# Six weight tiles between the latent attention's heads multiplied as split operands instead of as full f32

## The chip, the cores and the metric

The kernel runs on one core of a Trainium2 chip. The metric is the device time of one execution in microseconds; lower is better.

## What is computed

Two transformer layers on 256 tokens of width 1024, batch 1, all in f32. The first layer is a four-branch mixer with a SwiGLU; the second is a mixer of a RWKV-7 time mix, a latent attention (MLA, 4 heads) and a gated delta net, with a squared-ReLU feed-forward. The change lies in the second layer, in the projection of its input:

```python
u = _rms(h, ln_mix_g[l])
p = u @ w_in[l]                      # 1024 -> P_IN, here "in2"
p_rwkv, p_mla, p_gdn = _split(p, (RWKV_IN, MLA_IN, GDN_IN))
y_rwkv = rwkv7_time_mix(p_rwkv, ...)
y_mla = mla_attention(p_mla, ...)    # 4 heads, softmax over 256 keys
y_gdn = gated_deltanet(p_gdn, ...)   # causal conv of 4 taps, silu, then the delta rule
```

## The kernel before, in words

Weights come in chunks of 16 KB a partition through a ring of three slots (`rings`). A product of a 128-column tile of weights with the 256 tokens runs over eight blocks of 128 input channels (`KD` = 8). There are two ways to do one:

- **full f32**: `product_f` (L619 to L626), eight matmuls of 256 columns straight from the ring slot and from `HT`, the normalised input. In the trace each shows as two records of L625.
- **split**: `product3` (L660 to L671). Weights and input are each kept as a rounded high part and a remainder (low part), both in the faster operand type fp32r, and each block takes three matmuls: high by high, high by low, low by high (L668). A split costs ScalarE one copy (the high part) and VectorE one subtraction (the low part) over all weights of the piece. `IN2_HIGH` and `IN2_LOW` hold the two parts of this layer's input.

The second layer's projection has seven chunks, `("in2", 0)` to `("in2", 6)`. Chunks 0, 1 and 2 are split in pieces of 2048 elements a partition. Chunks 3 to 6 are multiplied as full f32. Eight tiles, in chunks 4 and 5, belong to the delta net; a pair of tiles fills one PSUM bank and is one job. Six of them stand between the heads of the latent attention, as `filler(n)` with n from 0 to 5 (L1118 to L1125), so that TensorE has work while ScalarE and VectorE do a head's softmax. Chunk 5's last pair, `f_job("in2", 5, 1)`, follows the heads.

The order of work is written out by hand for each engine, and engines wait for one another on semaphores. What matters is this loop over `u` from `NU` to `NU + 4`; below, "turn 0" to "turn 4", with head 0 to 3.

- TensorE (L1130 to L1138): `filler(0)` ahead of the loop, then in each turn the scores of head u, the transposes of the probabilities of head u - 1 (L838), `filler(u + 1)`, and the values of head u - 1 (L844 to L846). After it come the spread rows (L1144), the last pair of tiles, and more.
- ScalarE (L1986 to L2007): in each turn the first tap of a convolution tile (L1664 stages a bank, L1693), the transposed probabilities of head u - 1 into SBUF (L1792), the exponentials of head u (L1782), the tanh of the convolution tile (L1701), and some small rows of the delta rule: Exp in turn 0, Ln in turn 1 (with a table load before it and one back to Exp behind), Exp in turn 2.
- VectorE (L2743 to L2754): in each turn the mask and row maximum of head u (`bias_scores`, L2370 and L2372), the other three taps of a convolution tile (L2252) and its product with the tanh (L2261), the division of head u - 1 (L2411, L2412), and rows of the delta rule (L2701 to L2725). Turn 0 has `key_factors` (L2731 to L2738) as well. After the loop the first instruction is L2757, which waits for the spread rows.

The later stretch that matters: TensorE builds the first matrices of the RWKV inverse (L1181 to L1209), VectorE masks them (L2966), and TensorE goes on (L1225, L1382).

Of the kernel before, what the change touches and what calls it, by code (L numbers as in the profile page):

```python
# [16 lines left out]
F32 = mybir.dt.float32  # L17
F32R = mybir.dt.float32r
I32 = mybir.dt.int32
ALU = mybir.AluOpType  # L20
# [193 lines left out]
def build(nc, x, weights, params, params2, consts, tables, rel_bias, norm_final, positions, table_dram, out):  # L214
    with ExitStack() as ctx:
# [5 lines left out]
        def sem(name):  # L221

            if name not in sems:
                sems[name] = ctx.enter_context(nc.semaphore(name))
            return sems[name]
# [9 lines left out]
        def over(name, place, at, shape):  # L235

            return nc.alloc_sbuf_tensor_at(name, [P] + shape, F32R, offset=places[place] + 4 * at)
# [20 lines left out]

        Y_RW_AT = (P2COL["uq"][0] + 7) // 8 * 8
        Y_RW_LOW, Y_MLA_LOW = over("Y_RW_LOW", "BIAS", Y_RW_AT, [3, S]), over("Y_MLA_LOW", "NF", 0, [2, S])  # L260
        OVER_HT, OVER_HN = over("OVER_HT", "HT", 0, [KD, S]), over("OVER_HN", "HN", 0, [KD, S])
        MIX_LOW = over("MIX_LOW", "ARENA", 17408, [KD, S])

# [162 lines left out]
        def wait_job_out(eng, job):  # L426

            j = JOB_AT[job]
            eng.wait_ge(sem(f"job_out{j % 4}"), j // 4 + 1)

        def piece_parts(k):

# [140 lines left out]
        def _(pe):  # L573
# [47 lines left out]
            def product_f(o, w, a, n=P, ks=range(KD)):  # L621

                for k in ks:
                    wait_operand(k)
                    ins = pe.matmul(o, w[:, k, a:a + n], HT[:, k, :], start=(k == 0), stop=(k == KD - 1))  # L625
                return ins  # L626
# [491 lines left out]
            def filler(n):  # L1118

                i, j, t = 4 + n // 4, n // 2 % 2, n % 2  # L1120
                w = chunk("in2", i, KD, 512)
                o = open_job(("in2", i, j)) if t == 0 else job_bank(("in2", i, j))
                ins = product_f(o[:, t * S:(t + 1) * S], w, (n % 4) * P)
                if t:
                    close_job(ins)  # L1125

# [440 lines left out]
        def _(act):  # L1567
# [362 lines left out]
            def shift_tiles(i, j, tiles):  # L1930

                shifts[0] += 1
                o = job_arrived(act, ("in2", i, j))
                k = len(stage_readers)
                act.wait_ge(sem(stage_readers[k - 2][0]), stage_readers[k - 2][1])
                stage_readers.append(("shift_by_dve", shifts[0]))
                n = len(tiles) * S
                act.activation(STG[:, k % 2, 0:n], o[:, 0:n], ACT.Copy)
                for n, rt in enumerate(tiles):
                    ins = act.activation(RZ[:, rt, :], o[:, n * S:(n + 1) * S], ACT.Copy, scale=one_minus_mu[:, rt:rt + 1])  # L1940
                job_out(ins, ("in2", i, j))
# [25 lines left out]
            def row_roots(name, rows, n, scale, eps):  # L1967

                o = fill_arrived(act, name)
                fill_out(act.activation(rows, o[0:HD, 0:n], ACT.Sqrt, bias=SMALL[eps][0:HD, :], scale=scale), name)  # L1970

            shift_tiles(3, 0, (8, 9))
            take_fill(("rw_g", 0), flat(GG[:, 0:2, :]), 512, 0.5)
            take_fill(("rw_g", 1), GG[:, 2, :], S, 0.5)
# [8 lines left out]
            for n, dst in enumerate((QTm, KTm)):  # L1983
                for b in range(2):
                    take_fill(("mla_T", 2 * n + b), flat(dst[0:QK, 2 * b:2 * b + 2, :]), 512, rows=QK)
            for u in range(NU, NU + MH + 1):  # L1986
                if NU < u < NU + MH:
                    conv_tap(u - NU + 7)
                if u > NU:
                    take_probs_T(u - 1)  # L1990
                if u < NU + MH:
                    exps(u)
                else:
                    conv_tap(11)
                if u > NU:
                    conv_tanh(u - NU + 7)
                if u == NU:
                    act.wait_ge(sem("sp_minus_abs"), 2)
                    act.activation(GSPT, GSPT, ACT.Exp).then_inc(sem("sp_exp"), 1)
                elif u == NU + 1:  # L2000
                    act.wait_ge(sem("sp_exp1"), 2)
                    act.activation(GSPT, GSPT, ACT.Ln).then_inc(sem("sp_ln"), 1)
                elif u == NU + 2:
                    act.wait_ge(sem("gdn_cumulated"), 1)
                    act.activation(EGCUM, GCUM, ACT.Exp)
                    act.activation(EKEND, GCUM[:, 0:P], ACT.Exp, bias=GCUM[:, P - 1:P], scale=-1.0)\
                        .then_inc(sem("gdn_rows"), 1)  # L2007
# [147 lines left out]
        def _(dve):  # L2155
# [201 lines left out]
            def bias_scores(u):  # L2357

                br, h = ALL_UNITS[u]
                dve.wait_ge(sem("scores_written"), u + 1)  # L2360
                if u >= 2:
                    dve.wait_ge(sem("probs_ready"), u - 1)
                o, s = BK[4 + u % 2], SB_[:, u % 2, :]
                if br == 0:
                    dve.tensor_tensor(s, o[:, 0:384], cst("ssd_mask"), ALU.add).then_inc(sem("scores_read"), 1)
                    return
                m = {1: HEAD_BIAS[:, h, :], 2: cst("causal"), 3: HEAD_BIAS[:, (0, 1, 4, 5, 2, 3, 6, 7).index(h), :],
                     4: cst("mla_mask")}[br]
                init = NSINK[:, h:h + 1] if br == 3 else 3e38
                dve.tensor_tensor_reduce(s[:, 0:P], o[:, 0:P], m[:, P:S], -1.0, init, ALU.add, ALU.min,  # L2370
                                         NEGM[:, u % 2, 0:1])
                dve.tensor_tensor_reduce(s[:, P:384], o[:, P:384], m, -1.0, init, ALU.add, ALU.min,  # L2372
                                         NEGM[:, u % 2, 1:2]).then_inc(sem("scores_read"), 1)
# [219 lines left out]
            def shift_tiles(i, j, tiles):  # L2593

                wait_job_out(dve, ("in2", i, j))
                o = STG[:, STAGED["in2", i, j] % 2, :]
                for n, rt in enumerate(tiles):
                    z = RZ[:, rt, 1:S]
                    ins = dve.scalar_tensor_tensor(out=z, in0=o[:, n * S:(n + 1) * S - 1], scalar=prm2("mu", rt), in1=z,
                                                   op0=ALU.mult, op1=ALU.add)  # L2600
                ins.then_inc(sem("shift_by_dve"), 1)
# [89 lines left out]
                                   bc(g4[:, :, HD - 1:HD], [P, 6, P]), ALU.subtract))  # L2691
            dve.tensor_tensor(E3[:, :, :], GM[:, :, :], LW[:, :, :], ALU.subtract).then_inc(sem("decay_sums"), 1)

            shift_tiles(3, 0, (8, 9))
            shift_tiles(3, 1, (10,))
            o = job_arrived(dve, ("in2", 3, 2))
            link(dve.tensor_copy(GAX, o[32:32 + RH, 0:S]))
# [45 lines left out]
            for u in range(NU, NU + MH + 1):  # L2743
                if u < NU + MH:
                    bias_scores(u)
                if u > NU:
                    conv_taps(u - NU + 7)
                    conv_out(u - NU + 7)
                if u > NU:
                    finish_head(u - 1)  # L2750
                delta_rule_rows(u)
                if u == NU:
                    key_factors()
# [515 lines left out]
```

## Time and profile before

| | before |
|---|---|
| median of 3 runs | 962.67 us (962.37 to 964.09) |
| the profiled execution | 964.36 us |
| its span in the trace | 962.6 us |
| TensorE matmul, busy | 940.6 us (98%) |
| VectorE, busy | 589.7 us (61%) |
| ScalarE, busy | 471.0 us (49%) |

The span runs from the first to the last instruction of the profiled execution; 1.76 us of its time lie around the span. Busy time of TensorE is a modelled figure: matmuls overlap, so the time between two starts says more than a duration.

### The profile page before, as it was taken

To read this page: it belongs to the slowest core of one execution; us is meant where nothing else is said; L and a number is where in the kernel's file an instruction comes from. 1 tells how busy PE (TensorE), PEld (TensorE's weight loads), DVE (VectorE), ACT (ScalarE), POOL (GpSimd) and SP (SyncE) were. 2 spreads that over 40 slices of the span, in tenths; PEclk is the share of its full clock that TensorE was granted. 3 is DMA by queue.
4 is the path that set the end of the run, shared out by engine and by line. 5 is a ranking of instruction groups with operands and counts; after the bars stand their busy time and mean duration, and the time that the engine had idled before them with its cause. 6 is when DMAs were issued, how large, how long until landed. Compare 5 with 4: busy or idle time off the path is not lost.

```text
span 962.6 us, 16894 instructions
## 1 busy us (share of the span) xinstructions
PE 940.6 (98%) x7147; PEld 832.6 (86%) x7147; DVE 589.7 (61%) x931; ACT 471.0 (49%) x706; POOL 62.9 (7%) x76
## 2 busy tenths in 40 slices
PE   6999999999999999999999999999999999999998
PEld 5999987787778789999988899788988789998886
DVE  4775445557678755555553749578777466665434
ACT  5644335546773454444443665456335455545331
POOL 1000000021003300000000010002260000000000
PEclk9999999999999999999999989999999999999999
DMA  9985552243446534455553442222000444455521
GB/s 354 203 319 196 193 198 101 91 142 143 159 176 253 195 113 175 176 186 191 197 208 123 176 154 89 89 88 88 4 2 3 175 176 175 176 184 190 217 109 44
DMA packets 14778, 149.86 MB, mean 156 GB/s; under 512 B 1696, under 2 KB 3872, under 8 KB 6128
## 3 DMA queue, kind: packets, MB, share of 16 engines
q1 hardware_dynamic: 12448, 139.65, 39.0%
q0 software_dynamic: 1296, 5.24, 2.9%
q10 hardware_dynamic: 960, 3.90, 1.0%
q8 instruction: 57, 0.93, 0.4%
q14 instruction: 17, 0.14, 0.0%
HBM read 144.59 MB, written 4.19 MB: 155 GB/s over the span
## 4 chain that ended last, share of the span: by engine, by line
PE 85%; DVE 6%; ACT 4%; issue 2%; POOL 1%; ACTq 0%; DVEq 0%; POOLq 0%
PE bank L668 64%; PE bank L625 5%; PE bank L1382 3%; DVE W_LOW L2208 2%; ACT W_HIGH L1643 2%; PE bank L797 1%; POOL HN L3087 1%; PE bank L838 1%; PE bank L875 1%; PE bank L1144 1%; DVE ARENA L2252 1%; DVE X L2514 1%; PE bank L1249 1%; DVE OUT_LOW L2208 0%; PE bank L634 0%
## 5 line engine op out<-in xcount | busy, mean ns | idle before, releaser
L2208 DVE TENSOR_TENSOR W_LOW<-weights,W_HIGH 128x2048 fp32r<-128x2048 f32 (+1 forms) x98 | 224.4, 2292 | 214.0 <-ACT W_HIGH L1643 214.0
L1643 ACT ACTIVATE W_HIGH<-weights 128x2048 fp32r<-128x2048 f32 (+1 forms) x98 | 186.7, 1907 | 264.7 <-PE bank L668 264.7
L668 PE MATMUL bank<-OVER_HT,W_HIGH 128*128 128x256 f32 x608 | 171.0, 281 | 0.3 <-DVE OVER_HN L2220 0.3
L668 PE MATMUL bank<-OVER_HT,W_LOW 128*128 128x256 f32 x608 | 170.5, 280 | 0.0
L668 PE MATMUL bank<-OVER_HN,W_HIGH 128*128 128x256 f32 x608 | 170.5, 280 | 0.0
L668 PEld LDWEIGHTS bank<-OVER_HT,W_HIGH 128*128 128x128 f32 x608 | 114.5, 188 | 1.0 <-issue 0.8
L668 PEld LDWEIGHTS bank<-OVER_HN,W_HIGH 128*128 128x128 f32 x608 | 114.5, 188 | 0.0
L668 PEld LDWEIGHTS bank<-OVER_HT,W_LOW 128*128 128x128 f32 x608 | 114.5, 188 | 0.0
L668 PE MATMUL bank<-W_LOW,HID_HIGH 128*128 128x512 f32 x200 | 77.9, 389 | 0.0
L668 PE MATMUL bank<-W_HIGH,HID_LOW 128*128 128x512 f32 x200 | 77.9, 389 | 0.0
L668 PE MATMUL bank<-W_HIGH,HID_HIGH 128*128 128x512 f32 x200 | 77.8, 389 | 0.0
L668 PE MATMUL bank<-FIRST_HIGH,W_HIGH 128*128 128x256 f32 x224 | 63.6, 284 | 1.9 <-DVE W_LOW L2208 1.4
L668 PE MATMUL bank<-FIRST_HIGH,W_LOW 128*128 128x256 f32 x224 | 63.4, 283 | 0.0
L668 PE MATMUL bank<-FIRST_LOW,W_HIGH 128*128 128x256 f32 x224 | 63.3, 282 | 0.0
L625 PE MATMUL bank<-HT,weights 128*128 128x256 f32 x240 | 55.4, 383 | 0.0
L668 PE MATMUL bank<-GATE_HIGH,FIRST_HIGH 128*128 128x512 f32 x128 | 52.5, 410 | 0.5 <-DVE RING_LOW L2348 0.5
L668 PE MATMUL bank<-RING_LOW,FIRST_HIGH 128*128 128x512 f32 x128 | 50.3, 393 | 0.0
L668 PE MATMUL bank<-GATE_HIGH,FIRST_LOW 128*128 128x512 f32 x128 | 50.2, 392 | 0.0
L625 PEld LDWEIGHTS bank<-HT,weights 128*128 128x128 f32 x240 | 44.5, 190 | 6.7 <-issue 0.7
L2348 DVE TENSOR_TENSOR RING_LOW<-weights,GATE_HIGH 128x1024 fp32r<-128x1024 f32 x32 | 40.7, 1272 | 11.9 <-ACT GATE_HIGH L1678 11.9
L668 PEld LDWEIGHTS bank<-FIRST_HIGH,W_HIGH 128*128 128x128 f32 x224 | 42.3, 189 | 3.3 <-DVE W_LOW L2208 1.8
L668 PEld LDWEIGHTS bank<-W_HIGH,HID_HIGH 128*128 128x128 f32 x200 | 37.5, 188 | 7.8
(509 smaller groups left out, 1887.4 us busy)
## 6 DMA issues: line engine op xcount, KB each, us to landing
weights<-weights_dram SPq DMA_DIRECT2D x63, 2048.0 KB, 7.9
bias_rows_dram<-ARENA POOLq DMA_DIRECT2D x1, 3072.0 KB, 40.9
weights<-weights_dram SPq DMA_DIRECT2D x2, 1024.0 KB, 5.9
BIAS<-params_dram ACTq DMA_DIRECT2D x1, 1997.0 KB, 14.5
weights<-weights_dram SPq DMA_DIRECT2D x1, 1664.0 KB, 6.8
weights<-weights_dram SPq DMA_DIRECT2D x1, 1584.0 KB, 6.9
X<-x_dram ACTq DMA_DIRECT2D x2, 512.0 KB, 4.3
HT<-bias_rows_dram POOLq DMA_DIRECT2D x1, 1024.0 KB, 10.9
```

The lines of the kernel that those rows point to most:

```text
L625: ins = pe.matmul(o, w[:, k, a:a + n], HT[:, k, :], start=(k == 0), stop=(k == KD - 1))
L668: ins = pe.matmul(o, left[a][k], right[b][k], start=(first and k == 0 and a + b == 0), stop=(last and k == n - 1 and a == 1))
L797: ins = pe.matmul(BK[4 + u % 2][:, c0:c1], q[:, q0:q0 + P], k[:, 0:n], start=True, stop=(br != 2))
L838: ins = pe.transpose(probsT_bank(u)[:, j * P:(j + 1) * P], PB_[:, u % 2, j * P:(j + 1) * P], ident)
L875: ins = pe.matmul(o[pb:pb + HD, c0:S], V[:, n, a:a + HD], PT_[:, u % 2, k0:k1], start=(n == 0), stop=(n == 1))
L1144: ins = pe.matmul(o[:, c * P:(c + 1) * P], at[0:HD, :], rows, start=True, stop=True)
L1249: ins = pe.matmul(o[pb:pb + HD, c * P:(c + 1) * P], a[:, c, h * HD:(h + 1) * HD], b[:, matrix(c, h), :], start=(n == 0), stop=(c == 0 and ...
L1382: ins = pe.matmul(o[b:b + HD, n * HD:(n + 1) * HD], left[b:b + HD, 4 * g + n, :], right[b:b + HD, 4 * g + n, :], start=True, stop=True)
L1643: act.activation(like_source(piece_parts(k)[0], k), piece_source(k), ACT.Copy).then_inc(sem("pieces_high"), 1)
L2208: dve.tensor_tensor(low, piece_source(k), high.bitcast(F32), ALU.subtract)\
L2252: ins = dve.scalar_tensor_tensor(out=a, in0=o[:, 0:S - d], scalar=w[tap], in1=a, op0=ALU.mult, op1=ALU.add)
L2348: dve.tensor_tensor(low, src, high.bitcast(F32), ALU.subtract).then_inc(sem("gate_split"), 1)
```

## The change

For tiles n = 0 to 5 (`IN_TILES` = 6) `filler(n)` uses `product3` instead of `product_f`. A tile's high part is copied by ScalarE into one of two buffers (`TILE_HIGH`, 1024 elements a partition each), its low part is written by VectorE over the tile's own weights in the ring slot.

```diff
+        IN_TILES = 6
+        TILE_HIGH = [over("TILE_HIGH0", "HN", 0, [KD, P]), over("TILE_HIGH1", "BIAS", Y_RW_AT, [KD, P])]
...
+        def in_tile(n):
+            slot = weight_slots("in2", 4 + n // 4)[0]
+            cols = slice(n % 4 * P, (n % 4 + 1) * P)
+            src, low = [t[:, :].rearrange("p (k n) -> p k n", k=KD)[:, :, cols] for t in (rings[slot], RING_LOW[slot])]
+            return TILE_HIGH[n % 2], low, src
+
+        def wait_tile_read(eng, n):
+            if n % 2:
+                eng.wait_ge(sem("jobs_written"), JOB_AT["in2", 4 + n // 4, n // 2 % 2] + 1)
+            else:
+                eng.wait_ge(sem("tiles_read"), n // 2 + 1)
...
@@ TensorE, filler(n)
-                ins = product_f(o[:, t * S:(t + 1) * S], w, (n % 4) * P)
+                if n < IN_TILES:
+                    pe.wait_ge(sem("tiles_split"), n + 1)
+                    ins = product3(o[:, t * S:(t + 1) * S], [[part[:, k, :] for k in range(KD)] for part in in_tile(n)[0:2]],
+                                   [[part[:, k, :] for k in range(KD)] for part in stream2])
+                    if t == 0:
+                        ins.then_inc(sem("tiles_read"), 1)
+                else:
+                    ins = product_f(o[:, t * S:(t + 1) * S], w, (n % 4) * P)
@@ ScalarE
+            def tile_high(n):
+                slot, turn = weight_slots("in2", 4 + n // 4)
+                act.wait_ge(sem(f"weights_in{slot}"), 16 * turn)
+                if n >= 2:
+                    wait_tile_read(act, n - 2)
+                high, _, src = in_tile(n)
+                act.activation(high[:, :, :], src, ACT.Copy).then_inc(sem("tiles_high"), 1)
+
+            for n in range(2):
+                tile_high(n)
             shift_tiles(3, 0, (8, 9))
...
             for u in range(NU, NU + MH + 1):
+                if u < NU + IN_TILES - 2:
+                    tile_high(u - NU + 2)
                 if NU < u < NU + MH:
                     conv_tap(u - NU + 7)
@@ VectorE
+            def tile_low(n):
+                dve.wait_ge(sem("tiles_high"), n + 1)
+                high, low, src = in_tile(n)
+                dve.tensor_tensor(low, src, high[:, :, :].bitcast(F32), ALU.subtract).then_inc(sem("tiles_split"), 1)
+
             shift_tiles(3, 0, (8, 9))
+            for n in range(2):
+                tile_low(n)
             shift_tiles(3, 1, (10,))
...
                 if u < NU + MH:
                     bias_scores(u)
+                if u < NU + IN_TILES - 2:
+                    tile_low(u - NU + 2)
                 if u > NU:
                     conv_taps(u - NU + 7)
```

Where this moves instructions shows at three places. In the changed kernel the lines are some tens higher (L1643 to L2007 become L1666 to L2043, L2252 becomes L2288, L2370 becomes L2406); `TILE_HIGH_57` and `_58` are the two buffers, `RING_LOW_50` and `_51` the ring slots of chunks 4 and 5.

TensorE, `filler(0)` and what follows it, before:

```order
L625 MATMUL bank<-HT,weights 128x256 [waits job_out1,weights_in1]
L625 MATMUL bank<-HT,weights 128x256 x7
L797 MATMUL bank<-ARENA 128x128 [waits fill_out7,fill_out6,scores_read,fill_out5,fill_out4]
L797 MATMUL bank<-ARENA 128x256
L625 MATMUL bank<-HT,weights 128x256 [waits weights_in1]
```

and in the changed kernel, the first of eight blocks and the next tile's start:

```order
L684 MATMUL bank<-IN_HIGH,TILE_HIGH_57 128x256 [waits tiles_split,job_out1,weights_in1]
L684 MATMUL bank<-IN_LOW,TILE_HIGH_57 128x256
L684 MATMUL bank<-IN_HIGH,RING_LOW_50 128x256
...
L813 MATMUL bank<-ARENA 128x128 [waits fill_out7,fill_out6,scores_read,fill_out5,fill_out4]
L813 MATMUL bank<-ARENA 128x256
L684 MATMUL bank<-IN_HIGH,TILE_HIGH_58 128x256 [waits tiles_split,weights_in1]
```

Eight matmuls of a tile become 24, and each tile's first one waits for VectorE's subtraction. The scores keep their place.

ScalarE, from the Ln of turn 1 to the first convolution tap of turn 3, before (the last row is in turn 3):

```order
L2002 ACT_TABLE_LOAD
L2002 ACTIVATE SM<-SM 6x256
L1693 ACTIVATE ARENA<-bank,BIAS 128x256
L1792 ACTIVATE ARENA<-bank 128x384
L1782 ACT_TABLE_LOAD
L1782 ACTIVATE ARENA,STAT<-ARENA,STAT 128x128
L1782 ACTIVATE ARENA,STAT<-ARENA,STAT 128x256
L1701 ACTIVATE ARENA<-ARENA 128x256
L2005 ACTIVATE SM<-SM 6x256
L2006 ACTIVATE SM<-SM 6x128
L1664 ACTIVATE ARENA<-bank 128x512
```

and in the changed kernel:

```order
L2038 ACT_TABLE_LOAD
L2038 ACTIVATE SM<-SM 6x256
L2002 ACTIVATE TILE_HIGH_57<-weights 128x1024
L1716 ACTIVATE ARENA<-bank,BIAS 128x256
L1815 ACTIVATE ARENA<-bank 128x384
L1805 ACT_TABLE_LOAD
L1805 ACTIVATE ARENA,STAT<-ARENA,STAT 128x128
L1805 ACTIVATE ARENA,STAT<-ARENA,STAT 128x256
L1724 ACTIVATE ARENA<-ARENA 128x256
L2041 ACTIVATE SM<-SM 6x256
L2042 ACTIVATE SM<-SM 6x128
L2002 ACTIVATE TILE_HIGH_58<-weights 128x1024
```

The copy of the next tile but one comes first in each turn, ahead of the tap, of the transposed probabilities and of the exponentials; the copies of tiles 0 and 1 stand ahead of the loop.

VectorE, turn 1, before:

```order
L2370 ISA ARENA,STAT<-bank,CST 128x128
L2370 ISA STAT 128x1
L2372 ISA ARENA,STAT<-bank,CST 128x256
L2372 ISA STAT 128x1
L2252 SCALAR_TENSOR_TENSOR ARENA<-ARENA,BIAS 128x255
```

and in the changed kernel:

```order
L2406 ISA ARENA,STAT<-bank,CST 128x128
L2406 ISA STAT 128x1
L2408 ISA ARENA,STAT<-bank,CST 128x256
L2408 ISA STAT 128x1
L2734 TENSOR_TENSOR RING_LOW_50<-weights,TILE_HIGH_58 128x8x128
L2288 SCALAR_TENSOR_TENSOR ARENA<-ARENA,BIAS 128x255
```

The subtraction stands behind the row maxima and ahead of the taps, in each of turns 0 to 3. POOL's and SP's instructions do not move.

## Rows read from the trace of the kernel before

**Rows 1.** The page: busy us of each engine, its share of the span, its instructions

```profile
PE 940.6 (98%) x7147; PEld 832.6 (86%) x7147; DVE 589.7 (61%) x931; ACT 471.0 (49%) x706; POOL 62.9 (7%) x76
```

**Rows 2.** Windows around the loop: window, then busy us of PE, PEld, DVE, ACT, POOL, granted clock

```profile
609.00:621.10 12.10, 12.10 (x82) 8.90 (x81) 1.65 (x4) 5.68 (x12) 0.00 (x0) 1.00 0.42 154
621.10:645.20 24.10, 24.10 (x138) 21.69 (x137) 17.93 (x57) 14.86 (x39) 0.00 (x0) 1.00 0.26 98
645.20:674.80 29.60, 27.70 (x260) 23.35 (x259) 26.58 (x56) 17.27 (x39) 6.25 (x9) 1.00 0.19 73
```

**Rows 3.** Timeline of TensorE: start, us, instruction; a split product's 24, then fillers 0 and 1

```profile
570.91 0.28 PE L668 MATMUL bank<-IN_HIGH,W_HIGH 128*128 128x256 f32 x1
...
573.67 0.28 PE L668 MATMUL bank<-IN_HIGH,W_LOW 128*128 128x256 f32 x1
...
616.70 3.62 PE L625 MATMUL bank<-HT,weights 128*128 128x256 f32 x16
...
620.81 3.62 PE L625 MATMUL bank<-HT,weights 128*128 128x256 f32 x16
```

**Rows 4.** Lines L1678 and L2348: copy and subtraction of 1024 elements, ns min/median/max

```profile
L1678 ACT ACTIVATE GATE_HIGH<-weights x32: 1040/1057/1062, 136.2 to 270.6; 128x1024 fp32r<-128x1024 f32 x32
L2348 DVE TENSOR_TENSOR RING_LOW<-weights,GATE_HIGH x32: 1214/1224/1777, 139.2 to 274.4; 128x1024 fp32r<-128x1024 f32 x32
```

**Rows 5.** Timeline of VectorE: its rows behind a wait [idle before <-releaser], and one more

```profile
612.43 0.48 DVE L2599 SCALAR_TENSOR_TENSOR ARENA<-ARENA,BIAS 128x255 f32<-128x255 f32 x1 [3.43 <-ACT ARENA L1940]
...
621.11 0.29 DVE L2370 CUSTOM_DVE_ANT_0 ARENA<-bank,CST 128x128 f32<-128x128 f32 x1 [4.86 <-PE bank L797]
...
626.06 0.28 DVE L2370 CUSTOM_DVE_ANT_0 ARENA<-bank,CST 128x128 f32<-128x128 f32 x1
...
628.61 0.42 DVE L2261 SCALAR_TENSOR_TENSOR ARENA<-ARENA 128x256 f32<-128x256 f32 x1 [0.48 <-ACT ARENA L1701]
...
629.52 0.17 DVE L2411 RECIPROCAL STAT<-STAT 128x2 f32<-128x2 f32 x1 [0.49 <-PE bank L846]
...
631.04 1.52 DVE L2252 SCALAR_TENSOR_TENSOR ARENA<-ARENA,BIAS 128x255 f32<-128x255 f32 x3 [0.16 <-ACT ARENA L1693]
...
634.30 0.42 DVE L2261 SCALAR_TENSOR_TENSOR ARENA<-ARENA 128x256 f32<-128x256 f32 x1 [1.75 <-ACT ARENA L1701]
...
638.19 1.52 DVE L2252 SCALAR_TENSOR_TENSOR ARENA<-ARENA,BIAS 128x255 f32<-128x255 f32 x3 [1.07 <-ACT ARENA L1693]
...
640.20 0.42 DVE L2261 SCALAR_TENSOR_TENSOR ARENA<-ARENA 128x256 f32<-128x256 f32 x1 [0.48 <-ACT ARENA L1701]
...
643.69 0.43 DVE L2261 SCALAR_TENSOR_TENSOR ARENA<-ARENA 128x256 f32<-128x256 f32 x1 [0.48 <-ACT ARENA L1701]
...
645.23 1.14 DVE L2757 TENSOR_TENSOR ARENA<-ARENA,bank 128x512 f32<-128x512 f32 x2 [0.59 <-PE bank L1144]
```

**Rows 6.** Timeline of ScalarE: the gap ahead of the loop, then turns 1 and 2

```profile
605.49 0.60 ACT L1938 ACTIVATE ARENA<-bank 128x512 f32<-128x512 f32 x1 [5.09 <-PE bank L625]
...
628.59 1.28 ACT L2002 ACT_TABLE_LOAD   x1
630.23 0.42 ACT L2002 ACTIVATE SM<-SM 6x256 f32<-6x256 f32 x1 [0.36 <-DVE SM L2711]
...
631.18 0.49 ACT L1792 ACTIVATE ARENA<-bank 128x384 f32<-128x384 f32 x1 [0.17 <-ACT ARENA L1693]
631.68 1.28 ACT L1782 ACT_TABLE_LOAD   x1
...
636.62 0.42 ACT L2005 ACTIVATE SM<-SM 6x256 f32<-6x256 f32 x1 [2.35 <-DVE SM L2718]
```

**Rows 7.** Who TensorE waited for from 597 to 675 us, longest: us, times, longest us

```profile
PE bank L1225 <- DVE ARENA L2966: 1.3, 1, 1.3
```

**Rows 8.** Windows where TensorE's work was thin, columns as in rows 2

```profile
564.00:568.00 4.00, 4.00 (x20) 4.00 (x21) 0.00 (x0) 2.23 (x3) 0.00 (x0) 0.50 0.01 4
708.00:712.00 4.00, 2.51 (x68) 2.17 (x64) 2.61 (x6) 1.42 (x4) 2.25 (x4) 1.00 0.00 0
```

## The prediction

> **What bounds the kernel now.** I read the page first: TensorE is busy for 98% of the span, VectorE for 61% and ScalarE for 49% [rows 1]. That makes the change look like a plain gain, less TensorE time for work on engines with room. But these are shares of the whole span. So I read the windows around the attention loop next [rows 2]. From 621.1 to 645.2 us VectorE is busy 17.93 of 24.10 us and ScalarE 14.86. From 645.2 to 674.8 VectorE is busy 26.58 of 29.60 us, and TensorE then waits 1.3 us for VectorE at L1225 [rows 7], its longest wait from 597 us on. So in this part TensorE is only just the bound: VectorE's list is nearly as long. The third view, VectorE's timeline [rows 5], shows how near. At the loop's end VectorE waited only 0.59 us for TensorE (L2757, at 645.23). What it idled inside the loop it mostly idled for ScalarE.
>
> **What TensorE gains.** A full-f32 tile takes 3.46 us: 3.62 us of rows, less 0.16 of overlap, since the 16 records from 616.70 are followed at 620.15 by the next work, and the next such group starts at 620.81 [rows 3]. A split tile takes 24 matmuls. The first and the last of the 24 of a split product start at 570.91 and 573.67: they stand (573.67 - 570.91) / 23 = 0.120 us apart [rows 3], so a tile takes 24 x 0.120 = 2.88 us. The gain is 0.58 us a tile, 3.5 us for six. The Trainium skill ("TensorE: Matmul & The Clock Gate", Back-to-back issue gap) gives an isolated matmul at full clock N / 2.4 + 2.5 ns, 109 ns at 256 columns. By it, as an estimate, a tile would take 2.6 us. The rows at full clock show 120 ns, so the trace does not agree, and the sum takes the row; by the page's figure it would come out 0.3 us lower, as an estimate.
>
> **What ScalarE and VectorE pay.** Six copies and six subtractions of 1024 elements a partition. The nearest rows are the same two operations on the first layer's gate pieces: 1.06 us and 1.22 us, median of 32 each [rows 4]. Sources there are two runs of 512 elements; here they are eight runs of 128, 2 KB apart, which no row shows. From below, the same price; from above, the slowest of the 32 subtractions, 1.78 us. I take 1.0 us for a copy (its start-to-start share) and 1.25 for a subtraction, near the median, since nothing in the rows makes the stride dear. A hand-over between engines I take as 0.04 us.
>
> **Tiles 0 and 1: free.** ScalarE sits idle for 5.09 us before 605.49 [rows 6] and both copies fit there; chunk 4's weights have landed long before. VectorE sits idle for 3.43 us before 612.43 [rows 5] and two subtractions, 2.5 us, fit there. TensorE needs tile 0 at 616.70. If that cover were gone, `filler(0)` would be late by what sticks out.
>
> **Tiles 2 to 5: not free.** These four lie in turns 0 to 3. VectorE does 4 x 1.25 = 5.0 us more between 621.11 and 645.23. It starts 0.58 us earlier, since the scores of head 0 come after a shorter `filler(0)`. What can pay for the rest are the waits it has there [rows 5]: 0.48 + 0.49 + 0.16 + 1.75 + 1.07 + 0.48 + 0.48 + 0.59 = 5.5 us. The question is which of them last. Three (0.48 each) are the tanh of a convolution tile, which starts only when VectorE's taps end: these stay whatever happens. The 0.49 and the 0.59 are for TensorE, and go. The others hang on ScalarE's order, so I walked through the two lists with the durations above and those of the timelines, every instruction starting when its engine is free and its releaser done:
>
> - Turn 0. Row maxima at 620.5, tile 2's low part to 622.4, then `key_factors`; the next row maxima come at 626.8 where they came at 626.06 [rows 5].
> - Turn 1, and ScalarE's start of turn 2. Row maxima to 627.4, tile 3 to 628.7, taps to 630.2, tanh on ScalarE to 630.6. Only then does ScalarE load the Ln table (1.28 us [rows 6]), do the Ln (632.3), and copy tile 4 (633.3). Behind that copy stand the tap, the probabilities of head 1 into SBUF (done at 633.9, before at 631.67 [rows 6]), the second table load, and the exponentials of head 2.
> - Turn 2. VectorE waits 0.8 us for tile 4's copy, and 0.7 us for the tanh where it was 1.75. TensorE, ready for the values of head 1 at 631.5, gets them at 633.9: a stall of 2.4 us, and 0.9 us more for the next probabilities.
> - Turn 3. ScalarE does its two Exp rows when VectorE's scan is done, at about 639 (before 636.62 [rows 6]), then tile 5's copy to 640.6. VectorE waits 1.1 us for it; TensorE's values of head 2 stall 2.6 us, since their probabilities come behind that copy, and the next probabilities 0.3 us.
>
> VectorE's waits come to about 0.5 + 0.8 + 0.7 + 1.1 + 0.5 + 0.5 = 4.1 us in place of 5.5. So L2757 starts later by 5.0 - 0.58 - 1.4 = 3.0 us. TensorE's side gives the same from its own numbers: new stalls 2.4 + 0.9 + 2.6 + 0.3 = 6.2 us, less 3.5 us of shorter products: 2.7 us late at the spread rows. The two differ since VectorE need not wait 0.6 us at L2757 any more, and by roundings.
>
> **Behind the loop** nothing gives it back. TensorE's and VectorE's lists are both late by about the same, VectorE is 90% busy up to 674.8 [rows 2], and TensorE's 1.3 us wait at L1225 [rows 7] lasts. After that the chain is TensorE's again and slides whole. DMAs have cover: slots are freed a few us later, and the next chunks in them belong to the layer's output projection, well behind the delta net.
>
> **Sum:** +2.7 us on the profiled execution's 964.36 us (span 962.6, 1.8 us around it) gives 967.1. That execution lies 1.7 us above the median of the runs shown, 962.67, so against the median: **965.4 us**. About 0.2%, 1.9 us, is what a measurement of this kernel can tell from no change. Bounds of the unknown: with 1.78 us a subtraction the same walk gives +4.7; with 1.22 and 1.0, +2.6.
>
> **Rivals.**
>
> 1. *The splits are covered* (faster). VectorE's idle 5.5 us does hold 5.0 us of work, and by the page both helpers are far from full [rows 1]. If ScalarE's copies came into gaps (it idles 9 us in the loop [rows 2]) and no one waited for them, only TensorE's gain would count: -3.5 us, 959.2. Against: the copies stand at each turn's head, ahead of what TensorE waits for, and VectorE's end had 0.59 us to spare. It decides if the four subtractions delay L2757 by less than that. Chance 0.11.
> 2. *A draw*: the waits for ScalarE close up more than in my walk, leaving only the tanh waits, 4 x 0.48. VectorE's end then is late by 5.0 - 0.6 - 3.6 = +0.8 us, so 963.5, within 0.2%. For it: my walk carries some 30 hand-overs, each uncertain by 0.05. Chance 0.26.
> 3. *The clock falls.* At 564 to 568 us the granted clock was 0.50, 1.2 of 2.4 GHz, after TensorE had done 32-column products; from 708 to 712, with 2.51 us busy of 4 and waits between, it stayed at 1.00 [rows 8]. New stalls of 2.5 us are of the second kind. If the clock fell for some 7 us as it did there, about two tiles would double, +4 us on top: 969.4. The Trainium skill ("TensorE: Matmul & The Clock Gate", What's actually happening) says that the array is throttled by default and that activity releases it, which would let a stalled loop fall back; rows 8 show both outcomes. Chance 0.05.
>
> Slower as walked: 0.58.
>
> **How the numbers follow.** Faster by over 0.2%: rival 1, with 0.11. Within 0.2%: rival 2, with 0.26. Slower: 0.58 + 0.05 = 0.63. The range runs from 961.5 (a little of rival 1, which alone reaches 959.2) to 967.8 (most of the dear subtraction); outside are most of rival 1, the clock, and the tail of the price, together 2 in 10.
>
> **What the profile after would show.** Right: split tiles of 2.9 us on TensorE; copies near 1.0 and subtractions near 1.25 us; TensorE waiting for ScalarE's L1792 and L1782 (by their new numbers) some 6 us in all in the loop, where it waited for nothing; L2757 some 3 us later. Wrong if those waits are missing, or if VectorE still waits for TensorE at L2757; then rival 1 holds. A granted clock below 1 between 630 and 650 us would be rival 3. If the loop ends 3 us late and the span does not, something behind it had slack that I did not see.

## The result, and the profile after

| | before | after |
|---|---|---|
| first measurement, median (runs) | 962.67 us (7) | 967.09 us (7) |
| ratio after to before, 95% interval | | 1.0038 (1.0022 to 1.0053) |
| the same two kernels measured again (`c1`) | 965.04 us (22) | 967.74 us (12) |
| ratio, 95% interval | | 1.0025 (1.0013 to 1.0036) |
| the profiled execution, and its span | 964.36, 962.6 us | 966.05, 964.2 us |

The change makes the kernel slower, by 4.4 us between the medians of the first measurement (3.7 by the ratio, 2.1 to 5.1 by its interval) and by 2.7 us in the second, with its narrower interval of 1.3 to 3.5. The forecast was 965.4 us, within 961.5 to 967.8; the first measurement has 967.09.

The page after, the counterpart of [rows 1]:

```profile
PE 939.7 (97%) x7195; PEld 833.6 (86%) x7195; DVE 595.7 (62%) x937; ACT 477.5 (50%) x712; POOL 63.1 (7%) x76
```

VectorE has six instructions and 6.0 us more, ScalarE six and 6.5. TensorE has 48 records more (six tiles of 24 where there were 16) and 0.9 us less, although the new tiles save more than that. Where the rest went shows in the windows around the loop, columns as in [rows 2] (the last one is 3.2 us longer):

```profile
609.00:621.10 12.10, 12.10 (x102) 9.52 (x101) 4.48 (x12) 6.22 (x15) 0.00 (x0) 1.00 0.48 174
621.10:645.20 24.10, 21.08 (x149) 20.01 (x148) 19.27 (x52) 15.08 (x34) 0.00 (x0) 0.86 0.24 89
645.20:678.00 32.80, 30.87 (x330) 26.45 (x331) 29.29 (x64) 19.78 (x45) 6.25 (x9) 1.00 0.18 65
```

From 621.1 to 645.2 us TensorE was busy all 24.10 us before; now it is idle for 3.0 of them, and the granted clock, 1.00 before, is 0.86. Both points were in the prediction, the first as the forecast, the second as rival 3.

Whom TensorE waited for from 590 to 690 us (us in all, times, longest), to be held against [rows 7]:

```profile
PE bank L860 <- ACT ARENA L1815: 2.3, 1, 2.3
PE bank L1248 <- DVE ARENA L3012: 1.3, 1, 1.3
PE bank L854 <- ACT ARENA L1805: 0.7, 1, 0.7
```

L860 is the values of a head, L1815 its transposed probabilities on ScalarE; L854 and L1805 are the transposes and the exponentials. L1248 is L1225 before, with its 1.3 us unchanged. The waits of the loop are the two forecast for head 1 (2.4 and 0.9 us); those forecast for head 2 (2.6 and 0.3) are missing.

The two helpers' new instructions, ns min/median/max and span of the six:

```profile
L2002 ACT ACTIVATE TILE_HIGH<-weights x6: 1038/1062/1119, 598.7 to 638.0; 128x1024 fp32r<-128x1024 f32 x6
L2734 DVE TENSOR_TENSOR RING_LOW<-weights,TILE_HIGH x6: 1217/1222/1226, 607.4 to 639.1; 128x1024 fp32r<-128x1024 f32 x6
```

They cost what the contiguous ones in [rows 4] cost: eight runs of 128 elements, 2 KB apart, are not dear. VectorE's timeline (start, us, instruction, idle before it and its releaser), against [rows 5]:

```profile
607.36 2.35 DVE L2734 TENSOR_TENSOR RING_LOW<-weights,TILE_HIGH 128x1024 fp32r<-128x1024 f32 x2
610.88 0.48 DVE L2635 SCALAR_TENSOR_TENSOR ARENA<-ARENA,BIAS 128x255 f32<-128x255 f32 x1 [1.17 <-ACT ARENA L1963]
...
618.98 0.29 DVE L2406 CUSTOM_DVE_ANT_0 ARENA<-bank,CST 128x128 f32<-128x128 f32 x1 [4.29 <-PE bank L813]
...
628.76 0.42 DVE L2297 SCALAR_TENSOR_TENSOR ARENA<-ARENA 128x256 f32<-128x256 f32 x1 [0.48 <-ACT ARENA L1724]
...
631.43 1.23 DVE L2734 TENSOR_TENSOR RING_LOW<-weights,TILE_HIGH 128x1024 fp32r<-128x1024 f32 x1 [1.11 <-ACT TILE_HIGH L2002]
...
635.06 0.42 DVE L2297 SCALAR_TENSOR_TENSOR ARENA<-ARENA 128x256 f32<-128x256 f32 x1 [0.97 <-ACT ARENA L1724]
...
639.06 1.23 DVE L2734 TENSOR_TENSOR RING_LOW<-weights,TILE_HIGH 128x1024 fp32r<-128x1024 f32 x1 [1.19 <-ACT TILE_HIGH L2002]
...
646.45 1.13 DVE L2803 TENSOR_TENSOR ARENA<-ARENA,bank 128x512 f32<-128x512 f32 x2
```

The subtractions of tiles 0 and 1 (the first row) took up idle time: 3.43 us of it before the next tap have become 1.17. The last row is the old L2757 (645.23): it no longer waits for TensorE. The waits between the row maxima of head 0 and that row are 0.48, 1.11, 0.97, 1.19 and twice 0.48 us, 4.7 in all, where 4.1 were forecast and 5.5 stood before.

ScalarE's timeline in the same columns, from the Ln of turn 1 to the copy of turn 3, against [rows 6]:

```profile
628.75 1.28 ACT L2038 ACT_TABLE_LOAD   x1
630.04 0.41 ACT L2038 ACTIVATE SM<-SM 6x256 f32<-6x256 f32 x1
630.36 1.04 ACT L2002 ACTIVATE TILE_HIGH<-weights 128x1024 fp32r<-128x1024 f32 x1
...
631.93 0.49 ACT L1815 ACTIVATE ARENA<-bank 128x384 f32<-128x384 f32 x1 [0.17 <-ACT ARENA L1716]
632.44 1.28 ACT L1805 ACT_TABLE_LOAD   x1
...
637.37 0.41 ACT L2041 ACTIVATE SM<-SM 6x256 f32<-6x256 f32 x1 [2.35 <-DVE SM L2762]
...
637.99 1.04 ACT L2002 ACTIVATE TILE_HIGH<-weights 128x1024 fp32r<-128x1024 f32 x1
```

Tile 4's copy stands between the Ln and the probabilities of head 1, which TensorE's 2.3 us wait is for; they are 0.75 us later than in [rows 6], though the whole stretch started 1.55 us earlier.

**One measure for all traces.** Executions differ before the loop: the transposes ahead of it (L1115; `filler(0)` comes behind them) start at 614.91 us in the trace before, at 613.36 in the one after, and at 611.84 in a second trace of the changed kernel. So each trace is measured from there to the counterpart of L2757 ("loop") and to TensorE's start behind the wait at the counterpart of L1225 ("to L1225"), both in us; "walk" is what a walk through ScalarE's and VectorE's lists gave for the loop against before, in the prediction (by VectorE's list 3.0, by TensorE's 2.7) and in the expectations. The walks of the experiments were written down before each ran, but with the trace of the changed kernel already at hand.

| trace | loop | against before | walk | to L1225 | rest of the span |
|---|---|---|---|---|---|
| before | 30.32 | | | 59.88 | 287.8 |
| after | 33.09 | +2.77 | +2.7 to +3.0 | 62.63 | 288.2 |
| e1, two tiles | 29.38 | -0.94 | -1.2 | 59.09 | 288.2 |
| e2, splits without their use | 34.11 | +3.79 | +3.9 | 63.70 | 288.7 |
| e3, products alone | 28.76 | -1.56 | -1.8 | 58.31 | 288.8 |
| e4, four tiles | 32.29 | +1.97 | +1.3 | 61.85 | 288.8 |
| e5, kept running | 33.09 | +2.77 | | 62.65 | 288.8 |
| e6, subtractions on GpSimd | 37.23 | +6.91 | +0.4 | 66.80 | 289.2 |
| e7, four copies later | 35.83 | +5.51 | +5.3 | 65.39 | 289.1 |
| c1, the change again | 33.09 | +2.77 | | 62.65 | 289.2 |
| e8, kept running twice | 33.09 | +2.77 | | 62.65 | 289.2 |

By this table the two profiled spans differ by -1.55 (start) + 2.75 (to L1225) + 0.40 (rest) = 1.6 us. The middle term is the change's. As for the last one, the rest of the span is 0.4 to 1.4 us longer than before in every other trace, with longer and shorter loops alike; why is not shown.

### The profile page after: what moved, and what is told of

Same layout as the page of the kernel before. It is cut to its first block, busy times and chain, and to the rows that moved or that the text cites. A ratio compares the mean times of both kernels' runs of the same rounds, so it can differ in the third digit from the quotient of the medians.

```text
span 964.2 us, 17009 instructions
## 1 busy us (share of the span) xinstructions
PE 939.7 (97%) x7195; PEld 833.6 (86%) x7195; DVE 595.7 (62%) x937; ACT 477.5 (50%) x712; POOL 63.1 (7%) x76
## 4 chain that ended last, share of the span: by engine, by line
PE 83%; DVE 7%; ACT 5%; issue 2%; POOL 1%; ACTq 0%; DVEq 0%; POOLq 0%
PE bank L684 65%; PE bank L641 3%; PE bank L1405 3%; DVE W_LOW L2244 2%; ACT W_HIGH L1666 2%; POOL HN L3133 1%; PE bank L813 1%; PE bank L854 1%; DVE ARENA L2288 1%; PE bank L891 1%; PE bank L1167 1%; DVE X L2550 1%; PE bank L1272 1%; DVE OUT_LOW L2244 0%; PE bank L650 0%
## 5 line engine op out<-in xcount | busy, mean ns | idle before, releaser
L1666 ACT ACTIVATE W_HIGH<-weights 128x2048 fp32r<-128x2048 f32 (+1 forms) x98 | 186.7, 1907 | 262.6 <-PE bank L684 262.6
L684 PEld LDWEIGHTS bank<-W_HIGH,HID_LOW 128*128 128x128 f32 x200 | 37.5, 188 | 7.9
L684 PEld LDWEIGHTS bank<-W_LOW,HID_HIGH 128*128 128x128 f32 x200 | 37.5, 188 | 7.8
```

The costliest lines, as they stand in the source:

```text
L684: ins = pe.matmul(o, left[a][k], right[b][k], start=(first and k == 0 and a + b == 0), stop=(last and k == n - 1 and a == 1))
L1666: act.activation(like_source(piece_parts(k)[0], k), piece_source(k), ACT.Copy).then_inc(sem("pieces_high"), 1)
```

## The experiments

**One: two tiles only.** The free splits without the others.

```diff
-        IN_TILES = 6
+        IN_TILES = 2
```

> Only tiles 0 and 1 are split (IN_TILES = 2), whose copies and subtractions lie in gaps ahead of the loop. Theory 1 (the lists of VectorE and ScalarE inside the loop set its length): TensorE is 1.15 us shorter, nothing is added inside the loop, L2757's counterpart comes 1.2 us earlier after the first filler's start than in the kernel before, and the time is 1.2 us below the kernel before. Theory 2 (the clock's fall after the new stalls is the main price): no new stall, so no fall, the same 1.2 us gain. Theory 3 (the split product itself is slow in this place: operands out of the ring in 128-column pieces, or a switch between operand types): +0.3 to +1 us, two tiles at over 3.5 us each.

Measured: 964.39 us against 964.25, ratio 1.0005 (0.9993 to 1.0018). In the trace the loop is 0.94 us shorter and TensorE has no new wait. The splits of tiles 0 and 1 are free, and their gain shows in the trace of the loop. It does not show in the time: the interval, -0.7 to +1.7 us, leaves the 0.94 us just out. The mean granted clock of these runs was a little lower (0.995 in the median, 0.996 for the kernel before), which may hide it; whether the gain arrives at the end is open.

**Two: all splits, their result not used.** The products stay full f32; the copies and subtractions of the change are all made, each subtraction written over its own copy, and ScalarE waits for it before the buffer's next copy.

```diff
-                    ins = product3(o[:, t * S:(t + 1) * S], [[part[:, k, :] for k in range(KD)] for part in in_tile(n)[0:2]],
-                                   [[part[:, k, :] for k in range(KD)] for part in stream2])
+                    ins = product_f(o[:, t * S:(t + 1) * S], w, (n % 4) * P)
...
+                    act.wait_ge(sem("tiles_split"), n - 1)
...
-                dve.tensor_tensor(low, src, high[:, :, :].bitcast(F32), ALU.subtract).then_inc(sem("tiles_split"), 1)
+                dve.tensor_tensor(high[:, :, :], src, high[:, :, :].bitcast(F32), ALU.subtract).then_inc(sem("tiles_split"), 1)
```

> All six tiles are copied and subtracted as in the change, and TensorE waits for each, but multiplies them as full f32 out of the ring; the subtraction's result goes over the copy and is not used. Theory 1: the whole price without the gain, by the walk through the lists +3.9 us against the kernel before (1.2 us worse than the walk gave for the change, since head 0's scores come 0.6 us later and so on). Theory 2: TensorE is busier, its stalls are shorter (2.4 us less 0.6 or so each), and if the clock does not fall the time is below that of the change, near +2. Theory 3: the price is in the product, so +0.5 at most.

Measured: 968.05 us, ratio 1.0042 (1.0026 to 1.0059). TensorE's waits in its trace, as above:

```profile
PE bank L860 <- ACT ARENA L1814: 2.1, 2, 1.5
PE bank L854 <- ACT ARENA L1804: 0.7, 1, 0.7
```

The loop is 3.79 us longer: the price of the splits alone. With the shorter products it is 2.77. So six tiles that are each 0.58 us shorter bring 1.0 us of their 3.5.

**Three: the shorter products, without the splits of tiles 2 to 5.** Those four multiply what stands in the buffers of tiles 0 and 1, so the results are not the layer's; only the time is of use.

```diff
-                    pe.wait_ge(sem("tiles_split"), n + 1)
-                    ins = product3(o[:, t * S:(t + 1) * S], [[part[:, k, :] for k in range(KD)] for part in in_tile(n)[0:2]],
+                    pe.wait_ge(sem("tiles_split"), min(n + 1, 2))
+                    parts = in_tile(n)[0:2] if n < 2 else (TILE_HIGH[n % 2], TILE_HIGH[1 - n % 2])
+                    ins = product3(o[:, t * S:(t + 1) * S], [[part[:, k, :] for k in range(KD)] for part in parts],
...
-                if u < NU + IN_TILES - 2:
-                    tile_high(u - NU + 2)
...
-                if u < NU + IN_TILES - 2:
-                    tile_low(u - NU + 2)
```

> Tiles 2 to 5 are multiplied as three products of what is left in the two buffers of tiles 0 and 1; their own copies and subtractions are left out. Theory 1: all of the shorter products, nothing added in the loop: TensorE is 3.5 us shorter, but VectorE's and ScalarE's lists in the loop then set its end, so only 1.8 us are gained, not 3.5; TensorE shows some 1.7 us of new waits. Rival to it (TensorE alone bounds the loop): -3.5 us. Theory 3: no gain or a loss.

Measured: 962.18 us against 964.25, ratio 0.998 (0.997 to 0.999), 2.1 us between the medians and 1.56 us in the loop. TensorE's waits:

```profile
PE bank L860 <- ACT ARENA L1816: 1.2, 1, 1.2
PE bank L854 <- ACT ARENA L1806: 0.2, 1, 0.2
```

Even with four splits left out, the 3.5 us are not to be had: TensorE now outruns ScalarE, and the loop's end goes by the helpers' lists (VectorE no longer waits for TensorE there). Rival 1's 959.2 us was out of reach whatever the splits cost.

**Four: four tiles.**

```diff
-        IN_TILES = 6
+        IN_TILES = 4
```

> Four tiles are split (IN_TILES = 4): two inside the loop instead of four. Theory 1: +1.3 us against the kernel before, half of the way between two tiles (-1.2) and six (+2.7) or a bit over. Theory 2: the stall of turn 2 (tile 4's copy ahead of the probabilities) is gone or short, so the clock stays at 1.00 and the time is at most +0.5.

Measured: 965.69 us, ratio 1.0016 (1.0003 to 1.0029), loop +1.97 where the walk had +1.3. Tiles 4 and 5 are full f32 again, and at the loop's end VectorE waits for TensorE, 0.63 us in the row here and 0.59 us more at the old L2757:

```profile
644.57 0.17 DVE L2447 RECIPROCAL STAT<-STAT 128x2 f32<-128x2 f32 x1 [0.63 <-PE bank L862]
```

The granted clock has a part in this. The windows from 630 to 640 us:

```profile
630.00:635.00 5.00, 2.92 (x17) 2.22 (x16) 2.63 (x9) 3.87 (x10) 0.00 (x0) 0.92 0.77 265
635.00:640.00 5.00, 5.00 (x22) 4.19 (x21) 3.31 (x11) 3.20 (x10) 0.00 (x0) 0.73 0.37 156
```

Filler 4, full f32 here, starts at 634.21 us and took 5.30 us, where such a tile takes 3.62 with the clock up. Behind it TensorE has no wait up to the instruction that VectorE waits for (L862, at 644.15 us). It used the probabilities of head 2 at 639.35 us; ScalarE had them ready at 638.34. So with the clock up TensorE would have been some 1 us earlier from there on. That is an estimate from these rows, and more than the 0.7 us that the walk lacks; no execution of this kernel without the fall was traced.

**Five: is it the clock?** Ten idle products keep TensorE busy where it waits for the probabilities of head 1.

```diff
+                if u == NU + 2:
+                    keep_running(10)
```

> The change with 10 dummy 128-column f32 matmuls behind filler 3 (turn 2), where TensorE stalled 2.3 us for the probabilities of head 1: they last about 2.2 us, inside the stall. Theory 1: the loop's length does not hang on TensorE there, so the end of the loop is where it is in the change, or earlier by what the slow tile cost, 0 to 0.5 us. Theory 2 (clock): the granted clock stays at 1.00 from 634 to 641 us, filler 4 takes 2.9 us and not 5.1, and over the runs the time is 1 to 2 us below the change's, +2.7 against the kernel before.

Measured: 967.89 us against 963.62, ratio 1.0043 (1.0027 to 1.006); the gain of 1 to 2 us on the change that the clock theory asked for did not come. The windows from 634 to 641 us after the change, and here:

```profile
634.00:641.00 7.00, 6.29 (x31) 6.23 (x31) 4.71 (x15) 4.65 (x15) 0.00 (x0) 0.51 0.42 177
```

```profile
634.00:641.00 7.00, 4.33 (x34) 4.00 (x34) 4.81 (x14) 4.57 (x14) 0.00 (x0) 1.00 0.40 167
```

The clock stays up in this execution, and the loop takes the same 33.09 us. What changed is how TensorE spends that time. In the chain of waits after the change (start, us, engine, output, line), filler 4 takes 5.12 us, the next one 2.83:

```profile
635.67 5.12 PE bank L684 x24
...
641.85 2.83 PE bank L684 x24
```

With the clock up, in experiment five, it takes about 2.9, and the values behind it wait 2.1 us for their probabilities:

```profile
PE bank L860 <- ACT ARENA L1817: 2.1, 1, 2.1
PE bank L854 <- ACT ARENA L1807: 0.7, 1, 0.7
```

That is the wait of head 2 that the prediction had and the trace after lacks: TensorE at half clock filled it: its values of head 2 start at 640.59 us, 0.35 us behind the end of the copy of their probabilities.

**Six: the subtractions of tiles 2 to 5 on GpSimd,** which is idle in the loop.

```diff
-                if u < NU + IN_TILES - 2:
-                    tile_low(u - NU + 2)
...
+            for n in range(2, IN_TILES):
+                pool.wait_ge(sem("tiles_high"), n + 1)
+                high, low, tile = in_tile(n)
+                pool.tensor_tensor(low, tile, high[:, :, :].bitcast(F32), ALU.subtract).then_inc(sem("tiles_split"), 1)
```

> The change with the subtractions of tiles 2 to 5 on GpSimd (2.67 us each by its one row of this size in the trace before) instead of VectorE; ScalarE's copies stay. Theory 1: 5 us leave VectorE's list, the copies stay in ScalarE's: by the walk +0.4 us against the kernel before. If VectorE's part of the price is nothing and the copies' order is all, it stays at +2.7. If GpSimd and VectorE disturb one another, VectorE's instructions grow longer beside the GpSimd ones and the time lies above +1.

Measured: 972.47 us (6 runs), ratio 1.0082 (1.0059 to 1.0105): far dearer than the change, and the walk, +0.35 for +6.91, refuted. The timeline of GpSimd and VectorE shows most of it:

```profile
621.24 2.39 POOL L3157 TENSOR_TENSOR RING_LOW<-weights,TILE_HIGH 128x1024 fp32r<-128x1024 f32 x1 [49.62 <-ACT TILE_HIGH L2002]
...
621.29 2.49 DVE L2750 TENSOR_SCALAR SM<-SM 6x256 f32<-6x256 f32 x1
...
625.59 2.38 POOL L3157 TENSOR_TENSOR RING_LOW<-weights,TILE_HIGH 128x1024 fp32r<-128x1024 f32 x1 [1.96 <-ACT TILE_HIGH L2002]
625.70 3.08 DVE L2779 SCALAR_TENSOR_TENSOR ARENA<-ARENA 128x768 f32<-128x768 f32 x1
```

For comparison, the same two VectorE instructions after the change:

```profile
620.68 0.27 DVE L2750 TENSOR_SCALAR SM<-SM 6x256 f32<-6x256 f32 x1
...
622.88 0.96 DVE L2779 SCALAR_TENSOR_TENSOR ARENA<-ARENA 128x768 f32<-128x768 f32 x1
```

An instruction of VectorE that starts behind GpSimd's ends only after it: 0.27 us becomes 2.49, 0.96 becomes 3.08. It is the same in turns 2 and 3, where three taps take 3.37 and 2.87 us for 1.52. So VectorE is relieved of 1.2 us a tile and charged between 1.35 (2.87 - 1.52) and 2.2 us (2.49 - 0.27): 7.5 us in all for 4.9. That is 2.6 of the 4.1 us by which this loop is longer than the changed kernel's. VectorE's waits grew by 1.1 us as well, most of it for the first taps on ScalarE (1.47 and 2.02 us), and for 0.37 us it waited for TensorE at the end, where the clock was 0.66 from 645 to 650 us.

**Seven: ScalarE's order.** Four tiles, with the copy behind the exponentials in place of ahead of the tap.

```diff
-        IN_TILES = 6
+        IN_TILES = 4
...
             for u in range(NU, NU + MH + 1):
-                if u < NU + IN_TILES - 2:
-                    tile_high(u - NU + 2)
...
+                if u < NU + IN_TILES - 2:
+                    tile_high(u - NU + 2)
```

> Four tiles as in e4_four_tiles, the same work on each engine, but in each turn ScalarE's copy stands behind the exponentials instead of ahead of the tap. Theory 1 (order, not amount): VectorE's subtraction, and all behind it in its list, waits for the exponentials, so by the walk +5.3 us against the kernel before, 4 us worse than four tiles with the copy first. A theory of amounts alone (busy time added to busy engines) gives the same time as e4_four_tiles.

Measured: 969.47 us (6 runs), ratio 1.0056 (1.0034 to 1.0077), loop +5.51 where the walk had +5.27. It is the work of experiment four in another order, 3.5 us dearer in the loop. VectorE's two subtractions show where:

```profile
623.32 1.23 DVE L2734 TENSOR_TENSOR RING_LOW<-weights,TILE_HIGH 128x1024 fp32r<-128x1024 f32 x1 [2.00 <-ACT TILE_HIGH L2002]
...
631.49 1.23 DVE L2734 TENSOR_TENSOR RING_LOW<-weights,TILE_HIGH 128x1024 fp32r<-128x1024 f32 x1 [2.00 <-ACT TILE_HIGH L2002]
```

The exponentials depend on VectorE's row maxima, so a copy behind them comes a whole exchange later, and VectorE stands in front of its subtraction for 2.00 us. In four the copy was done before VectorE came to it.

**Eight: the change again, and with the clock held up in both gaps.** The second kernel has experiment five's line and ten idle products behind filler 4 as well:

```diff
+                if u == NU + 3:
+                    for _ in range(10):
+                        pe.matmul(job_bank(("in2", 5, 0))[:, S:S + P], ident, ident, start=True, stop=True)
```

> The changed kernel, once more, beside the next one on the same chip. The stretch from the first transposes to L2757 in its trace is 33.1 us as before (30.3 in the kernel before), +2.8. If falls of the clock outside this stretch make up the rest of the measured +3.7 to +4.4 us, the trace or the mean granted clocks of the runs (0.991 in the median, 0.996 in the kernel before) show more time at half clock than the loop's 7 us; if the clock has no part in it, the ratio falls to that of +2.8 us, 1.003.

> As e5_kept_running, and 10 dummy matmuls behind filler 4 as well, where the next stall (2.1 us, for the probabilities of head 2) came in that run's trace. If the rest of the loss over the lists' +2.8 us is the clock's fall after that second stall, the runs' median granted clock goes up to 0.996, and the time is +2.8 to +3.2 us against the kernel before. If it stays at +4.2, the rest is not the clock of this loop.

Measured side by side: the change 967.74 us, ratio 1.0025 (1.0013 to 1.0036); kept running twice 967.71 us, ratio 1.0026 (1.0015 to 1.0037). The windows of the change's second trace, then of the other kernel's:

```profile
629.00:634.00 5.00, 2.67 (x14) 1.96 (x15) 3.05 (x6) 4.30 (x9) 0.00 (x0) 0.81 0.87 308
634.00:641.00 7.00, 5.91 (x43) 5.57 (x43) 5.15 (x15) 4.50 (x13) 0.00 (x0) 0.89 0.19 81
```

```profile
629.00:634.00 5.00, 4.21 (x34) 3.62 (x33) 2.98 (x6) 4.37 (x10) 0.00 (x0) 1.00 0.90 301
634.00:641.00 7.00, 7.00 (x60) 6.82 (x60) 5.15 (x16) 4.44 (x13) 0.00 (x0) 1.00 0.21 88
```

Once the clock falls in the loop and once it does not; the loop is 33.09 us both times. Over the twelve runs of each, the mean granted clock rose from 0.9935 to 0.995 in the median, and the times are equal. With six tiles, the clock in the loop has no part in the price.

## Why the prediction was right, and where it was not

**TensorE's gain: right in size, in part out of reach.** Filler 0 of the changed kernel runs from 615.07 to 618.03 us in its trace, hand-over and all, and 24 products stand 0.120 us apart, so 2.88 us a tile. Of the 3.5 us for six, experiment three shows 1.6 in the loop as the most that it passes on. The prediction's remark that tiles of 2.6 us would lower the sum by 0.3 us counts one tile; on TensorE's side of the sum six make 1.6 (6 x 0.26), of which the first tile's share alone starts VectorE's list earlier.

**Copies and subtractions: right.** 1.06 and 1.22 us, for 1.0 and 1.25. The dear end, 1.78 us, did not occur.

**Tiles 0 and 1 free: right.** VectorE's idle time shrank from 3.43 to 1.17 us there, and ScalarE's 5.09 us gap to 3.19; experiment one has no price at all in the loop.

**Tiles 2 to 5 not free: right, by the mechanism named.** VectorE starts the loop's work early by the forecast 0.58 us: its first row maxima come 6.20 us behind the transposes before (621.11 - 614.91) and 5.62 after (618.98 - 613.36). Its waits go from 5.5 to 4.7 us (forecast 4.1), and the old L2757 comes 2.8 us later (forecast 3.0 by VectorE, 2.7 by TensorE). TensorE's stalls for head 1 are 2.3 and 0.7 us for 2.4 and 0.9. Experiment two isolates the price of the splits, 3.79 us for the walk's 3.9, and experiment seven moves one instruction a turn and gets 5.51 for 5.3.

**The stalls of head 2: not in the trace after, for a reason that the prediction had put elsewhere.** They were forecast at 2.6 and 0.3 us; the trace has none. The granted clock fell to 0.51 instead, filler 4 took 5.12 us in place of 2.9, and ended about when the probabilities came. With the clock up (experiment five) the wait is there, 2.1 us. Rival 3 is thus half right: the clock fell in both traces of the changed kernel, so a chance of 0.05 for the fall was far too low, but its step "+4 us on top" is wrong. It added the slow tiles to stalls that the slow tiles replace. Here 2 us of slowness fell on an engine that would have waited 2.1 us, and were free. In experiment four, where the slow tile was a full-f32 one and the wait behind it would have been shorter, part of it most likely was not.

**Behind the loop nothing gives it back: right.** The 2.77 us are 2.75 at the counterpart of L1225, and its own wait is 1.3 us as before.

**The sum.** Against the median it was +2.7 us. The second measurement has 2.7, the traces' loops 2.8, the first measurement 4.4, 1.7 above the forecast. No term of the walk is behind that 1.7: kernels with the same 33.09 us loop came out at 967.09 to 967.89 us, and the kernel before at medians of 962.67 (also over seven runs), 964.25, 963.62 and 965.04. So 967.09 lies 1.7 us above the 965.4 by the low level of the kernel before in that measurement, and the range held it by 0.7 us; with the level of the second measurement the same +2.7 gives 967.7, which is what was measured there. The kernel before's single executions in these measurements reach from 960.8 to 968.4 us. They go with the granted clock: over its 73 runs beside the experiments, each held against the mean of its own measurement, an execution is 0.8 us longer for each 0.001 that its mean granted clock is lower (correlation -0.81). Whether that carries the 1.7 us is not shown.

**Rivals 1 and 2.** Rival 1's condition, subtractions that delay L2757 by less than 0.59 us, failed by the 2.8. Rival 2, the draw, needed the waits for ScalarE to close up to the tanh waits alone; two waits for copies (1.11 and 1.19 us) and 0.5 us of a tanh that came late behind one stayed. What none of the rivals had is a subtraction put where it is not in VectorE's way; experiment six tried that and fell to another resource.

**A better version** was not found. Two tiles are 0.9 us shorter in the loop and equal in time (1.0005). Not tried: a third buffer for high parts, so that tile 2 is split in the idle time ahead of the loop as well.

## What to carry to other kernels

Judge work moved to helpers by the stretch in which it lands, not by the page's shares: here VectorE, busy for 61% of the span, had 0.6 us to spare at the loop's end, and ScalarE, busy for 49%, made both others wait. Write out the two lists with the durations of the trace and walk them, with every exchange between the helpers in it; six walks of seven came within 0.7 us of the traced loop (one of them, the prediction's, made before the result), and the one that failed took two engines as independent that were not. Copies for later work belong where an engine idles already, not at a turn's head ahead of what the main engine waits for, and not behind an exchange either.

## What the runs showed of the hardware

**A VectorE instruction beside GpSimd's waits for its end.** In experiment six every subtraction on GpSimd (2.35 to 2.39 us, about twice VectorE's 1.22) held up one VectorE instruction to GpSimd's own end: a TENSOR_SCALAR of 6x256 from 0.27 to 2.49 us, a SCALAR_TENSOR_TENSOR of 128x768 from 0.96 to 3.08. The Trainium skill ("SBUF — State Buffer", Who interferes with whom) has the rule: the two engines share a pair of SBUF ports, the first to issue holds it for its whole instruction, and VectorE needs it for two SBUF inputs or in its two-port modes. The trace agrees for the SCALAR_TENSOR_TENSORs, which read two SBUF inputs. For the TENSOR_SCALAR, which reads one, it agrees if that ran in a two-port mode, which no row here shows. That an instruction with one SBUF input outside those modes goes free, as the page says, no row here shows, since none that is known to be such fell beside a subtraction. Nor does a row show VectorE holding GpSimd.

**The same program, another clock.** From 634 to 641 us the changed kernel was granted 0.51 in one execution and 0.89 in another, where from 629 to 634 it was 1.00 and 0.81. The fall came after TensorE had waited 2 to 3 us with little to do. The length of a wait does not tell the falls from the rest: in experiments two and five, whose longest waits were 1.5 and 2.1 us, the clock was 1.00 through the loop, and in experiment four it fell to 0.50 behind waits of 1.4 and 0.7 us. The prediction had read the window from 708 us [rows 8] as showing that such waits leave the clock alone. That was one execution: in the second trace of the changed kernel the clock is 0.65 from 710 to 712 us and 0.50 from 712 to 714, behind the same thin stretch, where the kernel before had 1.00. What that later fall costs is not shown; the rest of the span is 289.2 us there and 288.8 in experiment five, which has no fall at that place.
